# Layer 2's conditioning slabs in the first block's w_up stage: weighted and added over row blocks by VectorE, with homes of their own

## The reference, cut to what matters

```python
c_act, cc_act = silu(c), silu(c_ctx)                 # 1024 each
for li in range(2):
    mod   = c_act  @ w_ada[li] + b_ada[li]           # w_ada[li]: 1024 x 6144
    mod_c = cc_act @ w_ada[li] + b_ada[li]
    sh1, sc1, g1, sh2, sc2, g2 = split(mod, 6)       # mod_c likewise
    x  = x  + g1 * mixer(modulate(rms_norm(x), sh1, sc1) @ w_in[li])
    x  = x  + g2 * conv_ffn(modulate(rms_norm(x), sh2, sc2), w_up[li], ..., w_down[li])
    # the context xc the same way in layer 0; in layer 1 only its keys, values and states
```

## Time and profile before

| | us |
|---|---|
| median of 3 runs | 1930.21 |
| lowest, highest | 1920.79, 1933.95 |
| profiled execution, its own time | 1927.21 |
| span of the profiled execution | 1925.3 |

### The profile page before, as it was taken

The page is one execution under the profiler, slowest core; times in us unless marked ns, Lnnn a source line. Parts: engine busy times, 40 slices in busy tenths (PEclk is TensorE's granted clock), DMA queues, the critical chain, the costliest instruction groups (busy, mean ns, idle before and its releaser), DMA issues.

```text
span 1925.3 us, 27917 instructions
## 1 busy us (share of the span) xinstructions
PE 1823.5 (95%) x11564; PEld 1525.3 (79%) x11564; DVE 1038.1 (54%) x1456; ACT 847.3 (44%) x1223; POOL 91.5 (5%) x171
## 2 busy tenths in 40 slices
PE   5999989899999999998998889999999999999998
PEld 3777866677777778876777779977999979889877
DVE  1333377664544463552646657866556665455475
ACT  2342445433333343354354445554333445565563
POOL 0000012210000000010001200001000010000010
PEclk9999999999999999999998999999999999999999
DMA  9653100125445532235210365543566565555562
GB/s 301 208 181 131 66 1 2 40 92 174 153 155 175 175 102 85 98 115 175 66 44 1 110 196 163 190 164 121 173 182 192 156 192 170 175 165 164 175 122 65
DMA packets 211596, 260.77 MB, mean 135 GB/s; under 512 B 4673, under 2 KB 173299, under 8 KB 211215
## 3 DMA queue, kind: packets, MB, share of 16 engines
q1 hardware_dynamic: 207850, 247.69, 39.7%
q0 software_dynamic: 3232, 11.15, 2.7%
q10 hardware_dynamic: 389, 0.15, 0.0%
HBM read 257.84 MB, written 1.12 MB: 135 GB/s over the span
## 4 chain that ended last, share of the span: by engine, by line
PE 74%; DVE 9%; DMA 6%; ACT 5%; issue 3%; SPq 1%; POOL 1%; DVEq 0%; ACTq 0%; POOLq 0%
PE acc L731 21%; PE acc L733 20%; PE acc L732 20%; DVE weights_low L1908 2%; PE acc L773 2%; ACT weights_high L1464 2%; DMA weights<-in_w_up_dram 2%; DMA weights<-in_w_in_dram 2%; PE acc L985 1%; DVE scratch L2087 1%; PE acc L1209 1%; POOL small L1346 1%; PE acc L714 1%; DMA weights<-in_w_down_dram 1%; DVE scratch L2433 1%
## 5 line engine op out<-in xcount | busy, mean ns | idle before, releaser
L1908 DVE TENSOR_TENSOR weights_low<-weights,weights_high 128x2048 fp32r<-128x2048 f32 (+1 forms) x184 | 416.9, 2269 | 575.1 <-ACT weights_high L1464 575.0
L1464 ACT ACTIVATE weights_high<-weights 128x2048 fp32r<-128x2048 f32 (+1 forms) x184 | 348.3, 1896 | 643.9 <-DMA weights<-in_w_up_dram 193.5
L731 PE MATMUL acc<-normed_t_high,weights_high 128*128 128x256 f32 (+1 forms) x1824 | 580.4, 318 | 15.0 <-DVE weights_low L1908 14.1
L733 PE MATMUL acc<-normed_t_high,weights_low 128*128 128x256 f32 (+1 forms) x1824 | 566.6, 311 | 0.0
L732 PE MATMUL acc<-normed_t_low,weights_high 128*128 128x256 f32 (+1 forms) x1824 | 566.6, 311 | 0.0
L731 PEld LDWEIGHTS acc<-normed_t_high,weights_high 128*128 128x128 f32 x1824 | 348.3, 191 | 43.8 <-DVE weights_low L1908 17.3
L732 PEld LDWEIGHTS acc<-normed_t_low,weights_high 128*128 128x128 f32 x1824 | 345.9, 190 | 24.7 <-issue 4.3
L733 PEld LDWEIGHTS acc<-normed_t_high,weights_low 128*128 128x128 f32 x1824 | 346.0, 190 | 21.1
L731 PE MATMUL acc<-weights_high,normed_t_high 128*128 128x512 f32 (+1 forms) x792 | 309.4, 391 | 6.9 <-DVE normed_t_low L2231 5.8
L733 PE MATMUL acc<-weights_high,normed_t_low 128*128 128x512 f32 (+1 forms) x792 | 305.4, 386 | 0.0
L732 PE MATMUL acc<-weights_low,normed_t_high 128*128 128x512 f32 (+1 forms) x792 | 305.3, 385 | 0.0
(11 more groups left out here) (247 smaller groups left out, 1826.3 us busy)
## 6 DMA issues: line engine op xcount, KB each, us to landing
weights<-in_w_up_dram SPq DMA_DIRECT2D x44, 1024.0 KB, 7.2
weights<-in_attn_w_in_dram SPq DMA_DIRECT2D x40, 1024.0 KB, 5.1
weights<-in_w_ada_dram SPq DMA_DIRECT2D x38, 1024.0 KB, 5.3
weights<-in_conv_w_in_dram SPq DMA_DIRECT2D x32, 1024.0 KB, 5.6
weights<-in_w_in_dram SPq DMA_DIRECT2D x24, 1024.0 KB, 7.4
weights<-in_w_down_dram SPq DMA_DIRECT2D x20, 1024.0 KB, 5.0
arena<-in_w_ada_dram SPq DMA_DIRECT2D x8, 1024.0 KB, 9.7
weights<-in_w_out_dram SPq DMA_DIRECT2D x8, 1024.0 KB, 5.0
```

Source lines behind the costliest of these rows:

```text
L731: pe.matmul(o, ah, bh, start=start, stop=False)
L733: return pe.matmul(o, al, bh, start=False, stop=stop)
L1464: act.activation(hi_slot(n)[:, 0:used], slot(n)[:, 0:used], ACT.Copy).then_inc(hi_in.sem, 1)
L1908: dve.tensor_tensor(slot(n, ring_lo)[:, 0:used], slot(n)[:, 0:used], hi_slot(n)[:, 0:used], ALU.subtract).then_inc(lo_in.sem, 1)
```

## The change

- `FILL` for layer 0's w_up stage keeps four slabs, (0, 20) to (0, 23). The other 16 (`BY_ROWS`, called slab j from 0 to 15) leave the plan and the ring.
- They get two homes of 2048 columns in `mg` (`ROWS_HOME`). SP issues slab j ahead of the w_up item that stands three plan positions behind item j + 1. For j of 0 and 1 it waits for the stage's norm, for the others until slab j - 2 has been summed (`rows_summed`).
- VectorE's `weighted_rows(j)` runs at item j + 2, behind `split_to`: for each of the eight row blocks it multiplies 256 columns by the partition's value of the conditioning vector and adds them to a row sum. With two streams (j below 8) it does so for both in turn, 16 instructions, each waiting for the last step but one; with one stream, 8 instructions, each waiting for the one before. The first is a tensor_scalar, the others are scalar_tensor_tensor. At the end it raises `rows_summed`. The sums lie in four homes in `arena`.
- TensorE's `sum_rows(j)` runs at item j + 4: it waits for `rows_summed`, and multiplies the row sum's two halves by a column of ones (four matmuls with two streams, two with one). VectorE's `add_sums(j)` adds the bias at the same item.
- The rows of (0, 20) to (0, 23) move to `early_rows`, in the home of `wf`, and POOL's load of `wf` for the second layer waits for the last gate sum.

```diff
-                ("w_up", 0): ([(0, n) for n in range(20, 24)] + [(1, n) for n in (*range(8), *range(12, 20))], [1] * 20),
+                ("w_up", 0): ([(0, n) for n in range(20, 24)], [1] * 4),
...
+        early_rows = scr[:, 3072:3584].rearrange("p (b n) -> p b n", b=2)
...
+        BY_ROWS = [(1, n) for n in (*range(8), *range(12, 20))]
+        ROWS_HOME = [mg[:, SLOT * n:SLOT * (n + 1)].rearrange("p (k n) -> p k n", k=KT) for n in range(2)]
+        ROWS_SUM = arena[:, FT * 512:FT * 512 + 1024].rearrange("p (b n) -> p b n", b=4)
+
+        def rows_streams(j):
+            return 2 if BY_ROWS[j][1] < 8 else 1
+
+        def rows_sum(j, s_):
+            n = sum(rows_streams(i) for i in range(j)) + s_
+            return n, ROWS_SUM[:, n % 4, :]
+
+        def rows_loads(n):
+            return [j for j in range(len(BY_ROWS)) if item["w_up", 0, (j + 1) // 2, (j + 1) % 2] + SLOTS == n]
+
+        def rows_slab(n, late):
+            return [n - late] if 0 <= n - late < len(BY_ROWS) else []
...
@@ block.tensor, ffn
+            def sum_rows(j):
+                pe.wait_ge(rows_summed.sem, rows_summed.after(j))
+                o = open_group(("sum", j))
+                for m in range(2):
+                    for s_ in range(rows_streams(j)):
+                        _, row = rows_sum(j, s_)
+                        c = rows_streams(j) * m + s_
+                        last = pe.matmul(o[:, c:c + 1], row[:, m * P:(m + 1) * P], ones, start=True, stop=True)
+                last.then_inc(full, 1)
...
+                        for j in rows_slab(2 * f2 + a, 4) if li == 0 else ():
+                            sum_rows(j)
@@ block.sync, the loop over the plan
                 if n >= SLOTS:
                     sp.wait_ge(*read_at[n - SLOTS])
...
+                for j in rows_loads(n):
+                    if j < 2:
+                        sp.wait_ge(full, full_after((("n2", 0), KT - 1)))
+                    else:
+                        sp.wait_ge(rows_summed.sem, rows_summed.after(j - 2))
+                    c0 = 256 * BY_ROWS[j][1]
+                    sp.dma_start(ROWS_HOME[j % 2], A["w_ada"][1, :, c0:c0 + 256].rearrange("(k p) n -> p k n", p=P)).then_inc(rows_in[j % 2], 16)
                 _, k, m = src.shape
                 sp.dma_start(slot(n)[:, 0:k * m].rearrange("p (k n) -> p k n", k=k), src).then_inc(slot_in[n % SLOTS], 16)
@@ block.gpsimd
+                    pool.wait_ge(full, full_after(("gb", 0, 23, 1)))
                     pool.dma_start(wf, A["w_fnet"][1, :, :].rearrange("(f p) n -> p f n", p=P)).then_inc(s_wf, 16)
@@ block.vector
+            def weighted_rows(j):
+                dve.wait_ge(rows_in[j % 2], 16 * (j // 2 + 1))
+                w = ROWS_HOME[j % 2]
+                streams = range(rows_streams(j))
...
+                for k in range(KT):
+                    for s_ in streams:
+                        _, row = rows_sum(j, s_)
+                        if k == 0:
+                            ins = dve.tensor_scalar(row, w[:, k, :], cond[:, k, s_:s_ + 1], None, ALU.mult)
+                        else:
+                            dve.wait_ge(vector_step, line.n - len(streams) + 1)
+                            ins = dve.scalar_tensor_tensor(row, w[:, k, :], cond[:, k, s_:s_ + 1], row, ALU.mult, ALU.add)
+                        ins.then_inc(vector_step, line.one())
+                dve.wait_ge(vector_step, line.n)
+                dve.sem_inc(rows_summed.sem, 1)
+            def add_sums(j):
+                li, n = BY_ROWS[j]
...
+                dve.wait_ge(full, full_after(("sum", j)))
...
+                dve.tensor_tensor(modt[:, li, m, 2 * q:2 * q + 2, :], sums, bb, ALU.add).then_inc(taken_of(key), 1)
...
+                        for j in rows_slab(2 * f2 + a, 4) if li == 0 else ():
+                            add_sums(j)
                         if 2 * f2 + a < FT - 1:
                             split_to(last_item(("w_up", li, f2, a), ("w_up", li), 2 * f2 + a) + SLOTS)
+                        for j in rows_slab(2 * f2 + a, 2) if li == 0 else ():
+                            weighted_rows(j)
```

More of the change, by code:

```diff
@@ L343, in program @@
                                      for t in range(first, NT)])
+        rows_in = [sem(f"row_weights_in{i}") for i in range(2)]
+        rows_summed = S("conditioning_rows_summed", range(16))
         c_ready, first_scale = sem("conditioning_padding_ready"), sem("first_norm_scale_ready")
@@ L507, in row_of @@
                 return start_rows[:, n, :]
+            if (li, n) in FILL["w_up", 0][0]:
+                return early_rows[:, n % 2, :]
             return extra_rows[:, n % 2, :] if (li, n) in EXTRA else grow[:, ADA_NO[li, n] % 2, :]
@@ L1972, in ada @@
                     dve.wait_ge(*taken_after(key))
+            def weighted_rows(j):
[3 more added lines that the diff above has]
+                for s_ in streams:
+                    n, row = rows_sum(j, s_)
+                    for i in range(j):
+                        if any(rows_sum(i, r)[0] == n - 4 for r in range(rows_streams(i))):
+                            dve.wait_ge(full, full_after(("sum", i)))
+                for k in range(KT):
+                    for s_ in streams:
+                        _, row = rows_sum(j, s_)
[9 more added lines that the diff above has]
+                li, n = BY_ROWS[j]
+                sec, q = n // 4, n % 4
+                m = {0: 0, 1: 1, 3: 2, 4: 3}[sec]
+                key = ("sum", j)
+                dve.wait_ge(full, full_after(key))
+                c0 = col["b_ada", li] + 2 * n
+                bb = cols[:, c0:c0 + 2].unsqueeze(2).to_broadcast([P, 2, 2])
+                if rows_streams(j) == 2:
+                    sums = bank(key, 4).rearrange("p (k s) -> p k s", s=2)
+                else:
+                    sums = bank(key, 2).unsqueeze(2).to_broadcast([P, 2, 2])
+                dve.tensor_tensor(modt[:, li, m, 2 * q:2 * q + 2, :], sums, bb, ALU.add).then_inc(taken_of(key), 1)
+                dve.wait_ge(*taken_after(key))
             def w_in(li):
```

## The result

The changed kernel takes 1991.53 us (median of four runs, 1991.12 to 1993.75) against 1932.08 us of the kernel before (four runs, 1920.79 to 1935.53): 1.0331 times the time, 95% interval 1.0304 to 1.0359, so slower by about 60 us. The profiled execution took 1991.12 us for a span of 1989.3.

The account below looks back on a forecast made before the run. TensorE's stream bounds the stage before; after, a loop of waits through SP's queue, 19.7 then 17.5 us a slab, moves the stage's end from 703.1 to 782.0: 1927.2 + 79, plus 1 towards the median, 2007 us; range 1985 to 2033.

Parts of the forecast that it names:

- the loop: Layer 0's w_up stage: slab end, SP's release, two transfers, high part, low part, next slab, in series; +79 us.
- TensorE's savings and sums: Layer 0's w_up stage: sixteen `ada` go, -27.0 us; sums add 14.6 us; TensorE alone would gain 12.4 us.
- VectorE's slab: `weighted_rows` on VectorE: 6.3 us a slab with two streams, 4.1 us with one.
- The size of a turn: Layer 0's w_up stage: one slab's passage through all links, 19.7 us with two streams, 17.5 with one.
- the pair of transfers: SP's queue: slab and item's weights, 1 MB each, land 9.1 us after the first issue; bounds 7.6 and 10.2.
- E(0): End of slab 0 on VectorE, the bracket giving the slab; forecast at 483.1 us, slab 1's at 506.6.
- The rest of the kernel: Rest of the diff, such as `early_rows`, POOL's wait and the layer-2 modulation: costed at nothing.
- The clock: TensorE after each wait in layer 0's w_up stage: lower clock adds 1.7 us an item, hidden inside 19.7.
- rival 1: Layer 0's w_up stage: two-stream steps of 0.52 us and landings 1 us slower; 2030 us, chance 0.17.
- Rival 2: TensorE in layer 0's w_up stage: 1.2 GHz for the whole item after each wait; about 2085 us, chance 0.07.
- rival 3: Layer 0's w_up stage: SP's wait already over, TensorE stays the bound; about 1915 us, chance 0.08.
- rival 4: Layer 0's w_up stage: VectorE the bound at 12.6 to 12.9 us for eight items; 1922 to 1928 us, chance 0.05.

Follow-up runs that it names:

- experiment 2: Changed kernel with only VectorE's order turned, weighted_rows ahead of split_to: 1907.08 us, ratio 0.9891 to the kernel before.
- experiment 3: Changed kernel with VectorE's order turned (weighted_rows ahead of split_to), repeated: 1907.71 us; with SP's item transfer also ahead of the slab's wait: 1906.04 us.
- experiment 1: Changed kernel with SP's order turned, the w_up item's transfer issued ahead of the slab's wait: 1914.92 us, ratio 0.9921 to the kernel before.
- experiment 4: Changed kernel with each slab issued one w_up item later, both orders as in the change: 1908.43 us, ratio 0.9884 to the kernel before.
- experiment 8: The kernel before, unchanged, profiled twice more to check for scatter outside the stage: 1926.47 and 1931.21 us.
- Experiment 6: Changed kernel with eight filler matmuls on TensorE ahead of each wait for a row sum: 1995.5 us, ratio 1.0365 to the kernel before.
- experiment 7: Changed kernel with VectorE's order turned and only the eight one-stream slabs by rows, the two-stream ones back on TensorE: 1924.52 us, ratio 0.9994.

## Why the prediction held, and where it was off

The direction, the mechanism and the range held: 1991.5 us lies in 1985 to 2033, and all of the loss is in the stage and the loop named. It was 15.5 us too high, and as a difference +77 us were forecast and +59.5 measured. Point by point:

- **TensorE's savings and sums.** Right in mechanism, too dear in the price of a sum: 0.9 and 0.45 us (experiments 2 and 3) for 1.14 and 0.69. The spreads of the earlier trace rows, two columns wide and on weights of the same size, were a near row but 0.2 us too dear; and half of their 1.04 us with 0.1 for changing over is 0.62, so that the 0.69 of the prediction has no row behind it (0.6 us over eight slabs). With the measured prices TensorE alone would gain 27.0 - 8 x 0.9 - 8 x 0.45 = 16.2 us; with the loop open the stage gains 13.6, and 2.0 us of waits for low parts are most of what is missing (experiment 3). In the changed kernel neither is seen.
- **VectorE's slab.** Right. Fourteen steps took 5.63 us, so they start (5.63 - 0.48) / 13 = 0.396 us apart, where 0.40 was taken from a single pair of starts in the earlier trace rows. Between 520 and 619 us a whole slab is 6.3 us. The one-stream steps are 0.52 apart ((3.61 - 0.48) / 6). By the Trainium skill, "VectorE: DVE Perf Modes", section "The DRAIN you can't avoid", where the next operation starts once the pipe is empty, a slab would take 16 x 0.48 = 7.7 us, an estimate. The same section lets an operation that is "not held" start earlier, and the trace has such starts: the next step begins 0.08 us before the end of the one before, behind a satisfied wait too.
- **The loop.** Right: the wait table of SP, the seven-step turn in the timeline, and experiments 1, 2 and 4, each of which cuts one of its conditions and turns +3.3% into -0.8 to -1.2%.
- **The size of a turn.** Forecast 19.7 and 17.5 us, measured 18.6 (505.80 to 598.72, five turns; the sixth two-stream turn took 19.55, its weights landing 1.0 us later) and 17.3 (618.27 to 722.10, six turns). The term that was off is the pair of transfers. It was taken as 9.1 us because the w_up slab stood 1.03 us behind the `ada` and landed 8.1 after its own issue. Released together, the two are issued 0.41 us apart, and in the two-stream turns the second lands a median 7.6 us after its own issue (7.6 to 8.6), 8.0 after the first. So the item's weights gained most of what they were issued earlier, down to near the lower bound of 7.6 that the prediction had named and not taken. In the one-stream turns they land by turns 7.8 to 7.9 and 8.7 to 9.6 us after their own issue, in the mean 8.9 after the first, and the term came nearly as forecast; why every second of those lands 1 to 2 us later is open.
- **The start and end of the chain.** E(0) and E(1) came at 483.62 and 505.80 us, in a kernel whose stage starts 2.3 us later by its first w_up issue (394.69 for 392.41); so 1.8 and 3.1 us earlier than forecast. From E(1) to E(7) 112.5 us for 118.2, from E(7) to E(13) 103.8 for 105.0, and the end 1.3 us earlier: together 11.3 us of the stage's +79.
- **The rest of the kernel.** Costed at nothing, in truth a gain of some 7 us (experiment 8), which is about what is left of the miss (77 - 59.5 - 11.3 = 6.2). The prediction had no term for stages that the change doesn't touch.
- **The clock.** Right that it is hidden: 0.86 and 0.88 instead of 1.00, TensorE busy 15.0 us of each 18.6 (90.38 of 112) where 14 was forecast. So its waits before the sums are 3.7 us in the mean (48.2 over 13) where some 7 were forecast: the slow matmuls fill the time that the loop leaves. Experiment 6 bought the clock back, and no time came with it.
- **Rivals 1 and 2.** Of rival 1 neither term came, the steps of 0.52 nor the slower landings in two-stream turns. Rival 2 wanted the low clock for a whole item; it was over within 6.5 us in the turn shown and within 10 in the one behind it, of 15 us of work.
- **Rivals 3 and 4.** Both describe what the kernel does once the loop is open. VectorE at 12.6 us an item is as rival 4 had it and did not bound TensorE in the second stretch; the total came out at 1906 to 1908, below both, by the cheaper sums and the gain elsewhere, and at 1915 in experiment 1, which is rival 3's number.

## What to carry to other kernels

When work moves to another engine, don't stop at the sum of each engine's time: follow each new wait into its queue, ask what stands behind it, and go on until the chain ends or comes back to where it began. If it comes back, the period is the sum of the links as soon as that is more than the fullest engine's work for a turn. The sign in a profile is that no engine is full and each names another as its releaser. In-order queues want urgent transfers ahead of those with a turn or two of slack; here one moved transfer is worth 77 us (1991.5 to 1914.9), and the change then gives 1% instead of taking 3%.

## What the runs showed of the hardware

- Two transfers of 1 MB issued 0.41 us apart were both there 8.0 to 8.3 us after the first issue in nine turns of the changed kernel, and 9.0 to 10.0 in four. With 1.03 us between the issues it was about 9.1. As the last of three, the item's weights took 10.2 to 11.4 us from their own issue (five items, issued 494.8 to 552.7 us, experiment 7).
- VectorE's 256-column steps of 0.48 us start 0.396 us apart over fourteen of them when each waits for the last but one, and 0.52 apart when each waits for the last.
- A one-column matmul on 128 x 128 float32 weights costs TensorE about 0.22 us (0.9 for four, 0.45 for two, changeover included; experiments 2 and 3).
- After a wait of 1.86 us before the sum, TensorE's granted clock was 0.74 over 6.5 us, so mixed of its two levels, 1.2 and 2.4 GHz, and 1.00 behind. After one of 4.71 us it was 0.53 and 0.50 over 6.5 us, so the lower level, 0.92 over the next 3.5 and 1.00 behind. Before, it was 1.00 over 103 us of this stage.
